# The pool branch's input weights multiplied once with its four 128x128 matrices, in block 1's routing

## The chip, the cores and the metric

The kernel runs on one core of a Trainium2 chip. The metric is the device time of one execution in microseconds. The core's engines run side by side, each with its own queue: TensorE (PE, with its weight loads as PEld), VectorE (DVE), ScalarE (ACT), GpSimd (POOL) and SyncE (SP). They wait for each other through semaphores. A matmul of 32-bit floats shows as two passes in the trace, one through plain transposes as one.

## The reference, cut to what matters

Two transformer blocks work on 1024 tokens of width 1024. Block 1 is a short-convolution mixer and an expert-choice layer: each of 16 experts takes the 128 tokens with the largest affinities. Block 2 is a mixer of two branches and a layer of 32 experts with two choices for each token. Between the blocks the rows are normalized and modulated again. The change concerns the second mixer's pool branch, 512 of its 2056 input columns:

```python
def pool_group(p, w_pool, b_pool, pool_scale):      # p = (h @ w_in)[..., COL_P:IN_COLS]
    ...
    pooled = (cs[:, 1:] - lo) / count[None, :, :, None] - pf
    y = jnp.einsum('bsgc,gcd->bsgd', pooled, w_pool)
    y = (y + b_pool) * pool_scale
```

`cs` is the running sum along the tokens. So each of four groups of 128 columns gets, at every token, the mean over the last 2, 4, 8 or 16 tokens less the token's own value, then a product with that group's 128x128 matrix, a bias and a scale. The pooling works along the tokens and the matrix along the columns, so the two can change places, and the matrix can be multiplied into the input weights.

## The kernel before, in words

The engines' programs are written out by hand, one queue each; every dependency is a counted semaphore. Matrix products are taken as three products of numbers split in two parts (`three`, lines 2513, 2514 and 2516), the parts made by ScalarE (a copy to the high part) and VectorE (the difference). Weights pass through `ring`, 12 slots of 128x1024 floats (512 KB), filled by SP in the order of use.

*Block 1's routing.* The logits of the 16 experts are done at the end of the first output stage. TensorE transposes the affinities (line 2702). VectorE then picks the 128 best tokens of each expert in 16 rounds of three instructions on 32 rows of 512 (lines 1856 to 1859), and signals `top_ready`. Meanwhile SP has loaded six sums over products with the second modulation weights into `xz[:, 2:8]` (line 596), and TensorE adds up their columns, 48 products with one column of ones (line 2526), each group of eight counted on `mod_mm`, up to 12. Then its queue goes on as follows:

```python
pe.wait_ge(S["top_ready"], 1 + past["top_ready"])
pe.transpose(ps[:, 2, 0:2 * E1], top_v[:], ident[0:2 * E1, 0:2 * E1])
pe.transpose(ps[:, 2, 2 * E1:4 * E1], top_f[:], ident[0:2 * E1, 0:2 * E1]).then_inc(S["topT_tr"], 1)
```

VectorE joins the two halves of the tokens (lines 1862 to 1877), GpSimd gathers the rows of the first two experts (line 815), TensorE transposes them (line 2722), and the first expert product starts. ScalarE has copied the first six expert weight chunks (line 1248) before, and does its row copy (line 1177) after the search. SP refills a ring slot when VectorE has split it (line 616).

*The second mixer.* Twelve input projections of 128 columns for all tokens (`n` = 0 to 11, chunks m = 4 to 15) run on TensorE; the work of four heads and the pool branch is put between their pieces by `between(n, k)`. Chunks 8 to 11 are the pool branch's columns of `w_in_2`. ScalarE copies such a projection into `tA` (line 1417), GpSimd makes the window sums and the difference (`pool_sums`, `pool_difference`, counted on `branch`), TensorE multiplies with the group's matrix (`pool_product`, line 2858), and VectorE adds the bias and scales (`pool_back`, line 2160). The four products stand here:

```python
if (n, k) in ((9, 2), (10, 2), (10, 5), (11, 2)):
    pool_product({(9, 2): 0, (10, 2): 1, (10, 5): 2, (11, 2): 3}[n, k])
```

The last projections (n = 8 to 11) are gates: ScalarE takes their sigmoid (lines 1424 and 1426), VectorE multiplies it in (line 2214). The output projection follows when all rows are there (`hy_done`, `pool_out`).

## Time and profile before

| | |
|---|---|
| time, three runs | 2093.75, 2094.17, 2098.7 us (median 2094.17) |
| profiled execution | 2094.59 us, span 2092.9 us |
| mean granted TensorE clock | 0.986 of full |
| busy share of the span | TensorE 96%, its weight loads 80%, VectorE 82%, ScalarE 59%, GpSimd 22% |
| routing of block 1 | from 435 to 484.6 us |
| block 1's experts | from 484.6 to 1036.8 us |
| second mixer's projections | up to 1299.4 us |

Times in the trace are microseconds from the span's start. A row of the timeline gives start, duration, engine, line, operation, output and inputs, and in brackets how long the engine was idle before and what released it. A count (x16) stands for instructions of one kind merged into a row.

### The profile page before, as it was taken

What the parts mean: (1) busy time and instruction counts of PE and PEld (TensorE: products, weight loads), DVE (VectorE), ACT (ScalarE), POOL (GpSimd) and SP (SyncE); (2) the same over time, 40 slices, a digit from 0 to 9 for tenths busy, and PEclk for the clock granted to TensorE, in tenths of its full rate; (3) what the DMA queues carried; (4) which work ended last, traced back from release to release, by engine and by line L of the source; (5) the groups of instructions that cost most, each with busy time, mean ns of one, the idle gap of its engine ahead of it and who ended that gap; (6) DMA issues with size and microseconds to landing.
All of it is one profiled execution on the core that took longest, in us unless ns stands there. A gap on an engine that the chain in (4) does not pass through costs nothing.

```text
span 2092.9 us, 31539 instructions
## 1 busy us (share of the span) xinstructions
PE 2013.9 (96%) x9666; PEld 1664.8 (80%) x9666; DVE 1707.5 (82%) x1929; ACT 1230.5 (59%) x1438; POOL 450.2 (22%) x370
## 2 busy tenths in 40 slices
PE   4999999968999999999999999999999999999997
PEld 4888887867888888888788887888888888887875
DVE  6575756588999999999865555658999999999996
ACT  5311103226888888888654533224888888888874
POOL 2000001101000000000010353111444444443443
PEclk9999999969999999999999999999999999999999
DMA  9476754358999999999821112356999999999997
GB/s 356 133 238 235 242 209 151 119 213 313 387 391 401 391 398 390 399 391 390 310 68 50 51 41 108 114 194 225 385 383 384 375 379 373 370 382 367 375 357 286
DMA packets 201559, 592.66 MB, mean 283 GB/s; under 512 B 24045, under 2 KB 61185, under 8 KB 201484
## 3 DMA queue, kind: packets, MB, share of 16 engines
q1 hardware_dynamic: 177632, 527.50, 66.3%
q0 software_dynamic: 22784, 61.46, 10.1%
q10 hardware_dynamic: 1068, 2.73, 0.3%
q8 instruction: 43, 0.70, 0.1%
q14 instruction: 32, 0.26, 0.0%
HBM read 561.10 MB, written 50.91 MB: 292 GB/s over the span
## 4 chain that ended last, share of the span: by engine, by line
PE 78%; DMA 9%; DVE 8%; ACT 2%; issue 2%; POOL 1%; DVEq 0%; POOLq 0%; ACTq 0%; SPq 0%
PE ps L2513 23%; PE ps L2516 23%; PE ps L2514 23%; DMA ring<-in_w_expert_up 6%; DVE mL L2337 2%; DMA ring<-in_ada_w 1%; PE ps L3038 1%; DMA ring<-in_w_expert_down 1%; PE ps L2634 1%; PE ps L2733 1%; DVE mL L2421 1%; PE ps L2722 1%; PE ps L2682 1%; ACT mH L1466 1%; PE ps L2858 1%
## 5 line engine op out<-in xcount | busy, mean ns | idle before, releaser
L2337 DVE TENSOR_TENSOR mL<-ring,mH 128x1024 fp32r<-128x1024 f32 x384 | 479.2, 1289 | 22.3 <-ACT mH L1466 20.8
L1884 DVE TENSOR_TENSOR mL<-ring,mH 128x1024 fp32r<-128x1024 f32 x384 | 456.5, 1222 | 19.0 <-ACT mH L1248 5.0
L1248 ACT ACTIVATE mH<-ring 128x1024 fp32r<-128x1024 f32 x384 | 401.8, 1060 | 97.3 <-PE ps L2516 86.9
L2513 PE MATMUL ps<-mH,xsH 128*128 128x512 f32 x1072 | 433.6, 404 | 2.8 <-DVE mL L2337 1.4
L1466 ACT ACTIVATE mH<-ring 128x1024 fp32r<-128x1024 f32 x384 | 394.9, 1056 | 65.6 <-PE ps L2516 23.7
L2514 PE MATMUL ps<-mL,xsH 128*128 128x512 f32 x1072 | 417.9, 390 | 0.0
L2516 PE MATMUL ps<-mH,xsL 128*128 128x512 f32 x1072 | 376.8, 391 | 0.0
L2516 PEld LDWEIGHTS ps<-mH,xsL 128*128 128x128 f32 x1072 | 201.2, 188 | 45.0
L2513 PEld LDWEIGHTS ps<-mH,xsH 128*128 128x128 f32 x1072 | 201.7, 188 | 41.5 <-DVE mL L2337 1.6
L2514 PEld LDWEIGHTS ps<-mL,xsH 128*128 128x128 f32 x1072 | 202.0, 188 | 37.3
L951 POOL TENSOR_TENSOR xz<-xz,gate_ffn_row 128x340 f32<-128x340 f32 (+1 forms) x93 | 162.9, 1756 | 239.5 <-DVE mL L2337 220.2
L2513 PE MATMUL ps<-mH,hidH 128*128 128x512 f32 x512 | 200.9, 392 | 1.3 <-issue 1.3
L2514 PE MATMUL ps<-mL,hidH 128*128 128x512 f32 x512 | 200.2, 391 | 0.0
L2516 PE MATMUL ps<-mH,hidL 128*128 128x512 f32 x512 | 158.5, 391 | 0.0
L2513 PE MATMUL ps<-hH,wH 128*128 128x512 f32 x384 | 151.4, 394 | 3.4 <-DVE hL L1636 2.4
L2514 PE MATMUL ps<-hL,wH 128*128 128x512 f32 x384 | 149.5, 389 | 0.0
L2516 PE MATMUL ps<-hH,wL 128*128 128x512 f32 x384 | 122.2, 389 | 0.0
L1582 DVE SCALAR_TENSOR_TENSOR acc<-ring,silu_c,acc 128x1024 f32<-128x1024 f32 x83 | 106.6, 1284 | 16.6 <-DMA ring<-in_ada_w 9.4
L2513 PEld LDWEIGHTS ps<-mH,hidH 128*128 128x128 f32 x512 | 96.8, 189 | 22.5 <-issue 1.9
L2516 PEld LDWEIGHTS ps<-mH,hidL 128*128 128x128 f32 x512 | 96.7, 189 | 20.3
L2514 PEld LDWEIGHTS ps<-mL,hidH 128*128 128x128 f32 x512 | 96.8, 189 | 20.0
L2513 PE MATMUL ps<-woH,zs 128*128 128x512 f32 x256 | 103.0, 402 | 4.1 <-DVE woL L1589 2.6
(507 smaller groups left out, 3139.2 us busy)
## 6 DMA issues: line engine op xcount, KB each, us to landing
ring<-in_w_expert_gate SPq DMA_DIRECT2D x140, 512.0 KB, 11.2
ring<-in_w_expert_up SPq DMA_DIRECT2D x140, 512.0 KB, 11.4
ring<-in_w_expert_down SPq DMA_DIRECT2D x140, 512.0 KB, 12.2
ring<-in_moe_w_gate SPq DMA_DIRECT2D x128, 512.0 KB, 6.4
ring<-in_moe_w_up SPq DMA_DIRECT2D x128, 512.0 KB, 6.3
ring<-in_moe_w_down SPq DMA_DIRECT2D x128, 512.0 KB, 7.6
ring<-in_ada_w SPq DMA_DIRECT2D x96, 512.0 KB, 7.0
ring<-in_sc_w_in SPq DMA_DIRECT2D x24, 512.0 KB, 8.7
```

Source lines behind the costliest of these rows:

```text
L951: pool.tensor_tensor(dst[:, at], src[:, at], gate_ffn_row[:, at], ALU.mult).then_inc(S["m2_row"], 1)
L1248: act.activation(mH[:, wset, :], ring[:, slot, :], ACT.Copy).then_inc(S["m1_hi"], 1)
L1466: act.activation(mH[:, wset, :], ring[:, slot, :], ACT.Copy).then_inc(S["m2_hi"], 1)
L1582: ins = dve.scalar_tensor_tensor(out=acc[:], in0=slot, scalar=silu_c[:, silu_col + k:silu_col + k + 1], in1=acc[:], op0=ALU.mult, op1=ALU.add)
L1884: dve.tensor_tensor(mL[:, wset, :], ring[:, slot, :], mH[:, wset, :].bitcast(F32), ALU.subtract).then_inc(S["m1_lo"], 1)
L2337: dve.tensor_tensor(mL[:, wset, :], ring[:, slot, :], mH[:, wset, :].bitcast(F32), ALU.subtract).then_inc(S["m2_lo"], 1)
L2421: dve.tensor_tensor(mL[:, c % WSETS, :], ring[:, c, :], mH[:, c % WSETS, :].bitcast(F32), ALU.subtract).then_inc(S["m2_lo"], 1)
L2513: pe.matmul(o, high, rh, start=start, stop=False)
L2514: pe.matmul(o, high, rl, start=False, stop=False)
L2516: last = pe.matmul(o, low, rh, start=False, stop=stop)
L2634: last = pe.transpose(ps[:, 4 + c // 4, (c % 4) * P:(c % 4 + 1) * P], xt[:, 1 - r, c * P:(c + 1) * P], ident[:])
L2682: last = pe.matmul(ps[0:2 * width, 7, 0:2 * P], rs[:, k, :], h2P[:, k, :], start=k == 0, stop=k == KD - 1)
```

## The change

The product of the pool branch's input weights (1024x512) with its four matrices is made once, on chip. After the column sums of block 1's routing, ScalarE loads the weights into `xz[:, 2:6]` (four transfers of 512 KB) and the matrices into `acc`. For each of the four groups TensorE transposes the eight 128x128 pieces, ScalarE copies them, TensorE multiplies them with the group's matrix, and ScalarE copies the result back over the weights. At the end ScalarE writes the 2 MB into a new DRAM tensor, `fold_dram`. TensorE waits for the last copy (`fold_ev`) before it goes on to `top_ready`. ScalarE waits for the write (`fold_out`) before the first expert's silu, which overwrites a part of `xz`; SP waits for it before it loads chunk 8.

In the second mixer the chunks 8 to 11 come from `fold_dram`. `pool_product`, its semaphore, its tile `wp` and GpSimd's load of the matrices are gone, and `pool_back` works in place on the window difference, as soon as GpSimd has made it. The rest of the diff shares the new semaphores with old ones.

```diff
--- before.py
+++ after.py
@@ -35,7 +35,7 @@
     silu_ready half_sum sq_done mod_ready tr_ready tr_hi split_hi f_part cv_done c_copied route1 e1_exp m1_used m1_hi
     m1_xT m1_xT_hi slots_ready m1_silu m1_hT m1_hT_hi if_zero gate_in if_hi v_even gate_exp branch d2_out uc_ready 
     q_mm pm_ready pv hn_tr num_out final_in dve_steps cols_tr mod_mm xn_done
-    tr_lo sums_out sums2_out sums_in row_cols row_tr row_copied rows_out rows_here c_here mid_tr tr_mid v_mm pool_steps neg_out mb_in mask_done exp_done small_ready small_exp sq_out intra_out kt_mm kw_out st_mm c_ready hd_out cell_w ov_l close_mm close_act close_dve last_root last_out m2_row m2_dst rows_known aff_ready halves_out affT_tr m1_xT_lo m1_hid m1_hT_lo if_lo v_odd if_mm pool_mm qk_mm qk_out s_mm
+    tr_lo sums_out sums2_out sums_in row_cols row_tr row_copied rows_out rows_here c_here mid_tr tr_mid v_mm pool_steps neg_out mb_in mask_done exp_done small_ready small_exp sq_out intra_out kt_mm kw_out st_mm c_ready hd_out cell_w ov_l close_mm close_act close_dve last_root last_out m2_row m2_dst rows_known aff_ready halves_out affT_tr m1_xT_lo m1_hid m1_hT_lo if_lo v_odd if_mm qk_mm qk_out s_mm
     hn_ready q_out
 """
 
@@ -100,6 +100,7 @@
     neg_dram = dram("neg_dram", [4, T])
     sums_dram = dram("sums_dram", [6, P, D])
     rows_dram = dram("rows_dram", [2, 4, D])
+    fold_dram = dram("fold_dram", [D, 4 * P])
 
 
     ring = sb("ring", [P, RING, D])
@@ -221,7 +222,6 @@
     tB = sb("tB", [P, T], scope=two)
     num = sb("num", [P, NT, P + 1], scope=two)
     cst = sb("cst", [P, NT - 1, P + 1], scope=two)
-    wp = sb("wp", [P, 4, P], scope=two)
     sm = sb("sm", [P, 2, 3, NT], scope=two)
     ms = sb("ms", [P, 8, NT], scope=two)
     gcol = sb("gcol", [P, 3, NT, 4], scope=two)
@@ -266,11 +266,12 @@
 
 
     lines = [
-        [("x1_done", NT), ("x1_done_2", NT)],
+        [("x1_done", NT), ("fold_out", 16), ("x1_done_2", NT)],
         [("sq2", NT), ("sq2_2", NT), ("sq_final", NT + 1)],
         [("var2", NT), ("var2_2", NT), ("var_final", NT + 1)],
         [("rstd2", NT), ("rstd2_2", NT), ("rstd_final", NT + 1)],
         [("h2_out", 16 * NT), ("h2_out_2", 16 * NT)],
+        [("sums_in", 96), ("fold_in", 16 * 5)],
         [("row_cols", 1), ("row_cols_2", 1)],
         [("row_tr", 1), ("row_tr_2", 1)],
         [("row_copied", 1), ("row_copied_2", 1)],
@@ -310,9 +311,10 @@
         [("sq_done", NT), ("sq_done_2", NT)],
         [("xn_done", NT), ("xn_done_2", NT)],
     ]
-    lines += [[(name, NT), (name + "_2", NT)]
-              for name in ("h2_done", "y_ready", "zs_hi", "zs_lo", "rt_done")]
-    lines += [[(name, NT + 1), (name + "_2", NT + 1)] for name in ("tr2", "h2T_ready")]
+    lines += [[(name, NT), (name + "_2", NT)] for name in ("h2_done", "zs_lo", "rt_done")]
+    lines += [[("y_ready", NT), ("fold_mm", 4), ("y_ready_2", NT)], [("zs_hi", NT), ("fold_ev", 4), ("zs_hi_2", NT)]]
+    lines += [[("tr2", NT + 1), ("fold_tr", 4), ("tr2_2", NT + 1)],
+              [("h2T_ready", NT + 1), ("fold_T", 4), ("h2T_ready_2", NT + 1)]]
     lines += [[(name, 2 * KD), (name + "_2", 2 * KD)] for name in ("tr_ready", "tr_hi", "tr_lo")]
     past = {}
     for line in lines:
@@ -442,6 +444,9 @@
     x1_tiles = x1_dram.rearrange("(t p) d -> p t d", p=P)
     h2_tiles = h2_dram.rearrange("(t p) d -> p t d", p=P)
 
+    fold_rows = fold_dram.rearrange("(k p) n -> p k n", p=P)
+    fold_w = xz[:, 2:6, :].rearrange("p u (k n) -> p (u k) n", n=4 * P)
+    fold_T, fold_by = xz[:, 6, :], acc[:, 0:4 * P].rearrange("p (h e) -> p h e", h=4)
     w_in2, w_out2 = (io[n].rearrange("(k p) n -> p k n", p=P) for n in ("w_in_2", "w_out_2"))
     m2_g, m2_u = (io[n].rearrange("e (p k) n -> e p (k n)", p=P) for n in ("w_expert_gate_2", "w_expert_up_2"))
     m2_d = io["w_expert_down_2"].rearrange("e (k p) n -> e p k n", p=P)
@@ -638,8 +643,10 @@
             sp.wait_ge(S["m1_lo"], 24 * E1 - NT + t + 1)
             sp.dma_start(x1_rows[t], x1_tiles[:, t, :]).then_inc(x_in[t], 16)
         for m in range(4, 16):
-            first = (0, FIRST_P, FIRST_O)[(m - 4) // 4] + (m % 4) * P
-            d2_chunk(m, w_in2[:, :, first:first + P], P)
+            first = (0, 0, FIRST_O)[(m - 4) // 4] + (m % 4) * P
+            if m == 8:
+                sp.wait_ge(S["fold_out"], 16 + past["fold_out"])
+            d2_chunk(m, (fold_rows if m // 4 == 2 else w_in2)[:, :, first:first + P], P)
         for k in range(KD):
             d2_chunk(16 + k, w_out2[:, k, :], D)
         sp.wait_ge(S["hy_done"], 4)
@@ -900,7 +907,7 @@
 
         pool.wait_ge(S["m1_lo"], 24 * E1)
         pool.wait_ge(S["tr_ready_2"], 16 + past["tr_ready_2"])
-        for dst, name in ((wq, "w_q_2"), (wk, "w_k_2"), (wp[:], "w_pool_2")):
+        for dst, name in ((wq, "w_q_2"), (wk, "w_k_2")):
             pool.dma_start(dst, io[name].rearrange("h d e -> d h e")).then_inc(S["cell_w"], 16)
         head_mask(0)
         for n in range(3, 9):
@@ -1264,6 +1271,19 @@
 
         for c in range(WSETS):
             m1_hi(0, 0, c)
+        act.wait_ge(S["mod_mm"], 12)
+        for u in range(4):
+            act.dma_start(fold_w[:, 2 * u:2 * u + 2, :], w_in2[:, 2 * u:2 * u + 2, FIRST_P:FIRST_P + 4 * P]
+                          ).then_inc(S["fold_in"], 16)
+        act.dma_start(fold_by, io["w_pool_2"].rearrange("h d e -> d h e")).then_inc(S["fold_in"], 16)
+        for g in range(4):
+            act.wait_ge(S["fold_tr"], g + 1 + past["fold_tr"])
+            act.activation(fold_T.rearrange("p (a b) -> p a b", a=2), ps[:, 4:6, :], ACT.Copy).then_inc(S["fold_T"], 1)
+            act.wait_ge(S["fold_mm"], g + 1 + past["fold_mm"])
+            act.activation(fold_w[:, :, g * P:(g + 1) * P], ps[:, 2:4, :].rearrange("p a (k n) -> p (a k) n", n=P),
+                           ACT.Copy).then_inc(S["fold_ev"], 1)
+        act.wait_ge(S["fold_ev"], 4 + past["fold_ev"])
+        act.dma_start(fold_rows, fold_w).then_inc(S["fold_out"], 16)
         row_copy("_2")
         act.wait_ge(S["slots_ready"], 1)
         for j in range(2):
@@ -1280,6 +1300,7 @@
                 if c in (14, 15) and not (static(q) and s >= E1 - 1):
                     x_hi(s + 1, 1 - r, c - 14)
                 if c == 5 and static(q) and s == 1:
+                    act.wait_ge(S["fold_out"], 16 + past["fold_out"])
                     swiglu_gate(0, 16)
                 if c == 21 and not (static(q) and s == E1):
                     swiglu_gate(s, n - 5)
@@ -2155,9 +2176,8 @@
                                      op0=ALU.mult, op1=ALU.add).then_inc(S["hd_out"], 1)
 
         def pool_back(g):
-            bank = 4 + 2 * (g % 2)
-            dve.wait_ge(S["pool_mm"], g + 1)
-            dve.tensor_scalar(xz[:, 4 + g, :].rearrange("p (a b) -> p a b", a=2), ps[:, bank:bank + 2, :],
+            dve.wait_ge(S["branch"], 5 + g)
+            dve.tensor_scalar(xz[:, 4 + g, :], xz[:, 4 + g, :],
                               col("b_pool_2", g), col("pool_scale_2", g), ALU.add, ALU.mult).then_inc(S["pool_out"], 1)
 
         dve.wait_ge(S["masks"], 7)
@@ -2704,6 +2724,19 @@
         pe.wait_ge(S["sums_in"], 96)
         for part in range(6):
             sum_columns(6 + part, xz[:, 2 + part, :])
+        pe.wait_ge(S["fold_in"], 16 * 5 + past["fold_in"])
+        for g in range(4):
+            if g:
+                pe.wait_ge(S["fold_ev"], g + past["fold_ev"])
+            for k in range(KD):
+                last = pe.transpose(ps[:, 4 + k // 4, (k % 4) * P:(k % 4 + 1) * P], fold_w[:, k, g * P:(g + 1) * P], ident[:])
+            last.then_inc(S["fold_tr"], 1)
+            pe.wait_ge(S["fold_T"], g + 1 + past["fold_T"])
+            for k in range(KD):
+                last = pe.matmul(ps[:, 2 + k // 4, (k % 4) * P:(k % 4 + 1) * P], fold_T[:, k * P:(k + 1) * P],
+                                 fold_by[:, g, :], start=True, stop=True)
+            last.then_inc(S["fold_mm"], 1)
+        pe.wait_ge(S["fold_ev"], 4 + past["fold_ev"])
         pe.wait_ge(S["top_ready"], 1 + past["top_ready"])
         pe.transpose(ps[:, 2, 0:2 * E1], top_v[:], ident[0:2 * E1, 0:2 * E1])
         pe.transpose(ps[:, 2, 2 * E1:4 * E1], top_f[:], ident[0:2 * E1, 0:2 * E1]).then_inc(S["topT_tr"], 1)
@@ -2869,7 +2902,7 @@
             last.then_inc(S["gate_cols"], 1)
 
         def pair_transposes():
-            pe.wait_ge(S["cell_w"], 48)
+            pe.wait_ge(S["cell_w"], 32)
             pe.wait_ge(S["gate_in"], 1 + past["gate_in"])
             pe.wait_ge(S["gate_rows"], 1 + past["gate_rows"])
             for u, w in enumerate((wq, wk)):
@@ -2943,16 +2976,6 @@
             for t in range(NT):
                 last = pe.transpose(ps[:, 6 + t // 4, (t % 4) * P:(t % 4 + 1) * P], num[:, t, 0:P], ident[:])
             last.then_inc(S["hn_tr"], 1)
-
-        def pool_product(g):
-            pe.wait_ge(S["branch"], 5 + g)
-            if g == 0:
-                pe.wait_ge(S["num_out"], 12)
-            elif g == 1:
-                pe.wait_ge(S["hd_out"], 4)
-            else:
-                pe.wait_ge(S["pool_out"], g - 1)
-            pair_matmul(4 + 2 * (g % 2), wp[:, g, :], xz[:, 4 + g, :]).then_inc(S["pool_mm"], 1)
 
         VALUES_AT, BACK_AT = ((1, 2, 3), (1, 4, 5)), {8: 2, 9: 6}
 
@@ -2975,8 +2998,6 @@
                 head_inputs(n - 3)
             if k == 7 and 0 <= n - 3 < 4:
                 head_keys(n - 3)
-            if (n, k) in ((9, 2), (10, 2), (10, 5), (11, 2)):
-                pool_product({(9, 2): 0, (10, 2): 1, (10, 5): 2, (11, 2): 3}[n, k])
 
         pe.wait_ge(S["ones_col"], 1 + past["ones_col"])
         for n in range(12):
```

## Rows read from the trace of the kernel before

**Rows 1.** The page's part 4, the chain that ended last, by engine.

```profile
PE 78%; DMA 9%; DVE 8%; ACT 2%; issue 2%; POOL 1%; DVEq 0%; POOLq 0%; ACTq 0%; SPq 0%
```

**Rows 2.** Timeline of block 1's routing, TensorE's rows.

```profile
442.31 20.64 PE L2526 MATMUL ps<-ones,xz 128*128 128x1 f32 x96 [6.07 <-DMA xz<-sums_dram]
472.93 0.31 PE L2708 MATMUL ps<-ident,top_v 32*128 32x32 f32 x1 [9.98 <-DVE top_f L1860]
473.75 1.01 PE L2713 MATMUL ps<-best,flip 128*128 128x16 f32 x4 [0.41 <-DVE best L1862]
474.77 4.90 PE L2521 MATMUL ps<-ones 128*128 128x128 f32 x28
...
484.62 0.50 PE L2513 MATMUL ps<-mH,xsH 128*128 128x512 f32 x1 [0.59 <-DVE xsL L1890]
```

**Rows 3.** Windows in the routing: length, busy by engine, granted clock, DMA share, GB/s.

```profile
440.00:445.00 5.00, 2.69 (x13) 2.69 (x13) 4.79 (x12) 1.22 (x2) 0.00 (x0) 0.50 1.03 419
...
463.00:472.90 9.90, 0.00 (x0) 0.00 (x0) 9.42 (x22) 0.00 (x0) 0.00 (x0) 0.50 0.00 0
```

**Rows 4.** Chain in order of time, end of the second mixer: start, duration, what.

```profile
1262.88 1.72 PE ps L2858 x4
...
1270.06 0.87 PE ps L2944 x8
...
1299.33 0.28 ACT tB L1426
```

**Rows 5.** Timeline of the second mixer's end on the other engines.

```profile
1267.09 1.23 DVE L2147 TENSOR_TENSOR num<-num,ms 128x1024 f32<-128x1024 f32 x1
...
1273.53 1.20 POOL L895 TENSOR_TENSOR xz<-edge,tA 128x16 f32<-128x16 f32 x1
...
1286.71 1.03 ACT L1424 ACTIVATE tA<-ps 128x1024 f32<-128x1024 f32 x1 [12.39 <-PE ps L2516]
...
1292.52 1.34 DVE L2160 TENSOR_SCALAR xz<-ps,cols 128x1024 f32<-128x1024 f32 x1 [6.06 <-PE ps L2858]
```

**Rows 6.** Instructions of line 904; groups of ScalarE by form, 1160 to 1300.

```profile
L904 POOL DMA_DIRECT2D wp<-in_w_pool x1: 772/772/772, 1078.0 to 1078.0; - x1
...
L1298 ACT ACTIVATE uH<-ring 128x1024 fp32r<-128x1024 f32 x7 | 7.6, 1089 | 6.7 <-PE ps L2516 6.7
```

**Rows 7.** Issues: ScalarE's at the opening, SP's from 1100, gathers of line 815.

```profile
2.35 1.02 ACTq L1083 DMA_DIRECT2D xz<-in_x  x2
...
ring<-in_w_in SPq DMA_DIRECT2D x7, 512.0 KB, 4.0
...
xt<-x_dram SPq DMA_DIRECT2D x1, 512.0 KB, 3.3
...
DMA to landing us min/median/max: 5.7/5.8/9.1
```

**Rows 8.** Timeline in the second mixer; the last row from its groups by form.

```profile
1196.14 1.96 PE L2858 MATMUL ps<-xz,ring 128*128 128x512 f32 x4
...
1198.14 1.03 ACT L1383 ACTIVATE ring<-ps 128x1024 f32<-128x1024 f32 x1 [7.13 <-PE ps L2858]
...
1199.33 1.03 PE L2898 MATMUL ps<-ident,xz 128*128 128x128 f32 x8
...
1213.03 1.95 PE L2906 MATMUL ps<-ring,xz 128*128 128x128 f32 x16
...
L1417 ACT ACTIVATE tA<-ps 128x1024 f32<-128x1024 f32 x5 | 5.3, 1067 | 3.4 <-POOL xz L895 3.4
```

**Rows 9.** Timeline of TensorE at the kernel's opening.

```profile
27.72 3.54 PE L2540 MATMUL ps<-ident,xz 128*128 128x128 f32 x16 [2.37 <-ACT xz L1111]
...
31.32 1.73 PE L2521 MATMUL ps<-ones 128*128 128x128 f32 x14
```

**Rows 10.** Window of block 1's experts (columns as above); waits in it: us, times, longest.

```profile
484.60:1036.80 552.20, 552.18 (x2552) 456.69 (x2552) 525.02 (x505) 441.67 (x457) 44.11 (x29) 1.00 1.01 384
...
ACT mH L1248 <- PE ps L2516: 86.9, 293, 2.0
```

## The prediction

> **What bounds the kernel now.** I read the page first, for its chain of work that ended last: TensorE is 78% of it, GpSimd 1% [rows 1]. So time is won or lost where TensorE's work changes while it is on that chain, or where the chain leaves TensorE and something new is put into it. The change does one of each, so I followed the chain in order of time through both places and then read the timelines there.
>
> The first place is block 1's routing, a serial stretch. VectorE searches for the largest affinities, round after round. TensorE does its 48 column sums beside the search, from 442.31 to 462.95, then idles 9.98 us, until VectorE's last result lets it transpose the winners at 472.93 [rows 2]. From there each step up to the first expert product at 484.62 waits for the one before. In the idle stretch the transfers stand still too [rows 3]: the ring of expert weights is full.
>
> The second place is the end of the second mixer. From 1262 to 1299 the chain is TensorE without a break, and the four pool products are four pieces of it, 1.72 us each, the first at 1262.88 [rows 4]. VectorE and ScalarE wait for TensorE there, not the other way round [rows 5].
>
> **The change, part by part.**
>
> *Removed: the four products.* Four pieces of 1.72 us on the chain are 6.9 us [rows 4]. What is late next? Transposing the last head's rows needs VectorE's result of 1268.32 (1267.09 + 1.23); TensorE would come to it at 1270.06 - 1.72 = 1268.34, just in time [rows 4, 5]. GpSimd's last window difference ends at 1274.7. ScalarE's third gate copy follows TensorE: three products earlier it starts at 1281.5 in place of 1286.71, and what VectorE and ScalarE do behind it (some 5 us) is done near 1286.5, while TensorE would end at 1299.33 - 6.9 = 1292.4 [rows 5]. So nothing takes the products' place. As a lower bound I let one of them (1.72) turn into a wait at the marginal transposes: 5.2 to 6.9 us, and I take 6.9. VectorE's four pool steps no longer wait for a product; that is worth nothing, since TensorE's projections cover it: VectorE idled 6.06 us before the last of them [rows 5].
>
> *Moved at no cost.* GpSimd's load of the pool matrices goes, 0.77 us of its issue [rows 6]; GpSimd is hardly on the chain, and were it, these 0.8 us would be the gain. The input chunks 8 to 11 come from the folded copy, in the same runs of 512 bytes; ScalarE's splits of such chunks waited for TensorE alone, never for a transfer [rows 6]. If that cover failed, one late chunk would cost up to the 4.0 us of its landing [rows 7]. SP's new wait there is for a write that will have ended hundreds of microseconds before.
>
> *Added: the loads.* ScalarE waits for all column sums, so nothing is issued before 463.0, with only the 9.9 us of the idle stretch left [rows 2]. Behind this wait on its queue stands its row copy, which follows the search anyhow. Five transfers go out; two issues of ScalarE's take 1.02 us [rows 7], so the last one leaves near 465.6. A lone 512 KB load lands in 3.3 us; at the 419 GB/s that the engines reach, its bytes are 1.25 of these, so some 2.0 us are fixed [rows 3, 7]. The four big loads (2.10 MB) take 5.1 us at 410 GB/s; the pool matrices (0.26 MB in runs of 512 bytes) take 1.0, since a chunk of twice that size in such runs lands in 4.0 us [rows 7]. That makes 463.1 + 2.0 + 5.1 + 1.0 = 471.2; I take 471.3. Bounds: everything at 419 GB/s gives 470.7; the slowest landing of the gathers, 9.1 us [rows 7], counted from the last issue, gives 474.7.
>
> *Added: the fold.* Its four groups run strictly one after another, because every hand-over is a wait: eight transposes, a copy of 128x1024, eight products of 128x128, another copy. The second mixer has each of them at full clock: transposes 1.03, copies 1.03 and 1.07, the sixteen passes of eight such products 1.95, hand-over to ScalarE 0.04 (1198.10 to 1198.14), back to TensorE 0.16 (1199.17 to 1199.33) [rows 8]. A group is 1.03 + 0.04 + 1.03 + 0.16 + 1.95 + 0.04 + 1.07 + 0.16 = 5.48 us. At half clock eight transposes cost 3.54 / 2 = 1.77 [rows 9] and a pass 20.64 / 96 = 0.215 [rows 2], sixteen of them 3.44; the group is then 7.71 us.
>
> Which clock? The granted clock is 0.50 in the idle stretch [rows 3], which is 1.2 GHz. After the search, the 28 passes from 474.77 took 4.90 us, 0.175 each: they began at half clock and ended at full [rows 2]. At the kernel's opening 16 transposes ran at half rate (0.22 each), and the 14 passes behind them at full (0.12) [rows 9]. So I take the first group at half clock and three at full: 7.71 + 16.44 = 24.2 us. Bounds: 21.9 (all full) and 30.8 (all half). The Trainium skill ("TensorE: Matmul & The Clock Gate", Part 4: PE-mode transpose) says that transposes do not bring the clock to its full level. By that only the products would help here, and the sum would lean to the slow rival below; the opening's rows speak against it.
>
> *The wait that this puts into the chain.* The fold ends at 471.3 + 24.2 = 495.5. On TensorE's queue the winners' transposes stand behind it, so they go from 472.9 to 495.5, 22.6 us later. For them wait VectorE's choice of tokens, ScalarE's row copy, GpSimd's gather and SP's refill of the ring, so all shift alike. Of the 9.9 us that the search still covers, the loads use 8.3.
>
> *After it.* The small products from 472.93 to 474.76 run at full clock: half of 1.01, and 0.1 on the two before, are 0.6 us gained [rows 2]. The folded matrix is written out (2.10 MB, some 5 us) just as the gather starts. Gathers in this stretch landed in 5.7, 5.8 and 9.1 us [rows 7], so 0 to 3.3 us more; I take 1.0, as most of the write is done before the gather's data moves. ScalarE's wait for that write, ahead of the first silu, is hidden behind 16 weight chunks of 552.2 / 384 = 1.44 us, 23 us of TensorE work [rows 10]; if it were not, the rest of the 5 us would show.
>
> *Sum*, against the profiled execution's own 2094.6: 22.6 - 0.6 + 1.0 - 6.9 = +16.1, 2110.7. The median shown, 2094.2, is 0.4 us lower; I say 2110.
>
> **The rivals.**
> - *The clock stays at half through the fold.* The copies leave TensorE idle 2.5 of a group's 7.7 us, and 20 us of column sums did not lift the clock [rows 2, 3]; the opening speaks against it. The fold is 30.8 us and the 0.6 is lost: 471.3 + 30.8 - 472.9 = 29.2, and 2094.6 + 29.2 + 1.0 - 6.9 = 2117.9. The skill's rule on transposes leads here.
> - *The clock is up from the first group*: 2.2 us less, 2108.5.
> - *The gather pays the whole 3.3* beside the write: 2113.0.
> - *The mixer's end does not move*, because another engine was as late as TensorE: 2110.7 + 6.9 = 2117.6. The waits of VectorE and ScalarE [rows 5] say no.
> - *Not slower: block 1's experts give the delay back.* If that stage waited for weights, a later start would find more of them ready, and only the mixer's gain would be left: 2087.7. It decides once the stage holds 16.1 us of TensorE idle time that weights cause. The trace has 0.02 us of idle time in 552.2, and ScalarE's weight copies wait for TensorE, 86.9 us in all [rows 10]; and with the ring full nothing can be fetched ahead.
>
> **How the numbers follow.** My forecast has 0.55, half clock 0.16, full clock from the start 0.11, the gather 0.09, the unmoved end 0.04, the delay given back 0.03, and 0.02 is for something unseen near no change. The unknowns at their ends together give 2094.6 + (470.7 + 21.9 - 472.9) - 0.6 - 6.9 = 2106.8 and 2094.6 + (474.7 + 30.8 - 472.9) + 3.3 - 5.2 = 2125.3. The far upper end needs every term at its worst, so I cut it, and give 2105 to 2119. A measurement of this kernel tells some 0.3%, 6 us, from no change. All the slow cases lie beyond that: slower 0.95, same 0.02, faster 0.03.
>
> **What would show it.** In the profile after: the last of the five loads landing near 471; transposes, copy, products, copy, four times between 471 and 495, the first round longer; the winners' transposes near 495 and the first expert product near 507; an experts' stage as long as before; no products between the pieces of the last projections, and a mixer some 6.9 us shorter. I am wrong if the fold ends before 480, if the experts' stage is shorter than its 552 us, or if the last projections wait for VectorE or GpSimd.

## The result, and the profile after

The changed kernel takes 2119.05 us (median of four runs, 2115.82 to 2121.23), 1.0111 times the kernel before (95% interval 1.0099 to 1.0124): some 23 us slower, where I forecast 16 and a range that ended at 2119. A fourth run of the kernel before, at 2279.01 us, is left out of the comparison as slow. The profiled execution was its fastest, 2115.82 us with a span of 2114.2, so 21.2 us over that of before.

The page's chain by engine, in answer to [rows 1]:

```profile
PE 77%; DMA 11%; DVE 7%; ACT 3%; issue 2%; POOL 0%; SPq 0%; ACTq 0%; DVEq 0%; POOLq 0%
```

The share of transfers has grown from 9% to 11%: in order of time the chain now passes through the fold's loads (the last one, of the matrices, for 6.9 us) and through a longer gather (9.2 us). The timeline of TensorE in the routing, in answer to [rows 2] (lines 2732 and 2736 are the fold's transposes and products, 2741 the winners' transposes, 2755 those of the gathered rows, 2533 the first expert product):

```profile
470.39 1.97 PE L2732 MATMUL ps<-ident,xz 128*128 128x128 f32 x8 [9.14 <-DMA acc<-in_w_pool]
473.47 3.78 PE L2736 MATMUL ps<-acc,xz 128*128 128x128 f32 x16 [1.11 <-ACT xz L1281]
478.37 1.10 PE L2732 MATMUL ps<-ident,xz 128*128 128x128 f32 x8 [1.11 <-ACT xz L1283]
480.57 3.31 PE L2736 MATMUL ps<-acc,xz 128*128 128x128 f32 x16 [1.11 <-ACT xz L1281]
485.00 1.09 PE L2732 MATMUL ps<-ident,xz 128*128 128x128 f32 x8 [1.11 <-ACT xz L1283]
487.20 2.05 PE L2736 MATMUL ps<-acc,xz 128*128 128x128 f32 x16 [1.11 <-ACT xz L1281]
...
495.74 0.24 PE L2741 MATMUL ps<-ident,top_v 32*128 32x32 f32 x1 [1.11 <-ACT xz L1283]
...
508.14 1.94 PE L2755 MATMUL ps<-ident,xz 128*128 128x128 f32 x8 [6.22 <-DMA xz<-h_dram,tok_in]
...
510.70 0.79 PE L2533 MATMUL ps<-mH,xsH 128*128 128x512 f32 x1
```

The four rounds are there: transposes, copy, products, copy, with 1.11 us of idle TensorE at every hand-over. They last from 470.39 to the winners' transposes at 495.74, 25.35 us. A round at half clock is 1.97 + 3.78 us of TensorE work, one at full clock 1.09 + 2.05. In this execution the second round is mixed: its transposes ran at full clock and most of its products at half. The winners' transposes come at 495.74, 22.8 us later than before. From them to the first expert product it is 14.96 us, where it was 11.69 [rows 2]. The windows show the granted clock (last but two of the columns) in the idle stretch, in the fold and in the gather's wait, then over the experts:

```profile
465.00:470.00 5.00, 0.00 (x0) 0.00 (x0) 4.76 (x12) 0.00 (x0) 0.00 (x0) 0.50 0.96 350
475.00:480.00 5.00, 3.35 (x19) 2.81 (x18) 0.00 (x0) 1.52 (x2) 0.00 (x0) 0.73 0.00 0
480.00:485.00 5.00, 3.31 (x17) 3.02 (x17) 0.00 (x0) 1.54 (x2) 0.00 (x0) 0.66 0.00 0
485.00:490.00 5.00, 3.14 (x24) 2.71 (x24) 0.00 (x0) 1.73 (x2) 0.00 (x0) 1.00 0.00 0
...
505.00:510.00 5.00, 1.86 (x9) 1.89 (x10) 0.04 (x1) 0.60 (x1) 0.00 (x0) 0.50 0.99 401
...
510.70:1063.30 552.60, 552.60 (x2554) 457.11 (x2552) 524.89 (x505) 441.58 (x458) 44.12 (x29) 1.00 1.00 382
```

The transfers that stood still between 463 and 472.9 [rows 3] now carry the loads. TensorE is busy in every microsecond of the experts' stage, as in [rows 10]: nothing is given back there. The clock is at half again when the gathered rows arrive (505 to 510): their eight transposes take 1.94 us and the first expert product 0.79, where it took 0.50 [rows 2]. The timelines of ScalarE and GpSimd, and the transfers issued from 495 to 511 (median us from issue to landing at the end):

```profile
461.29 2.17 ACTq L1276 DMA_DIRECT2D xz<-in_w_in  x4
...
495.72 0.38 ACTq L1286 DMA_DIRECT2D fold_dram<-xz  x1
...
498.83 1.84 POOL L822 DMA_INDIRECT xz<-h_dram,tok_in  x1 [0.54 <-DVE tok_in L1921]
...
1319.21 0.28 ACT L1447 ACTIVATE tB<-ps 128x128 f32<-128x128 f32 x1 [7.51 <-PE ps L2536]
```

```profile
fold_dram<-xz ACTq DMA_DIRECT2D x1, 2048.0 KB, 7.7
...
xz<-h_dram,tok_in POOLq DMA_INDIRECT x2, 9.4
```

The write is issued at 495.72 and lands 7.7 us later, at 503.4. The gather issued at 498.83 runs beside it, and TensorE can use its rows only 9.3 us after the issue. In the kernel before it was 6.0 us:

```profile
476.55 1.84 POOL L815 DMA_INDIRECT xz<-h_dram,tok_in  x1 [0.45 <-DVE tok_in L1900]
...
482.52 1.07 PE L2722 MATMUL ps<-ident,xz 128*128 128x128 f32 x8 [2.85 <-DMA xz<-h_dram,tok_in]
```

So the 3.3 us from the winners to the first expert product are 3.3 for the gather and 0.5 for what follows its rows at half clock, less 0.5 for the small products ahead of it. The mixer's end is the last copy of a gate, 1319.21. From the first expert product to it are 808.5 us, against 814.7 before [rows 2, 4]: 6.2 us gained.

### The profile page after: what moved, and what is told of

Same layout as the page of the kernel before. It is cut to its first block, busy times and chain, and to the rows that moved or that the text cites. A ratio compares the mean times of both kernels' runs of the same rounds, so it can differ in the third digit from the quotient of the medians.

```text
span 2114.2 us, 31729 instructions
## 1 busy us (share of the span) xinstructions
PE 2023.1 (96%) x9746; PEld 1676.5 (79%) x9746; DVE 1707.6 (81%) x1929; ACT 1238.3 (59%) x1446; POOL 451.5 (21%) x369
## 4 chain that ended last, share of the span: by engine, by line
PE 77%; DMA 11%; DVE 7%; ACT 3%; issue 2%; POOL 0%; SPq 0%; ACTq 0%; DVEq 0%; POOLq 0%
PE ps L2533 23%; PE ps L2536 22%; PE ps L2534 22%; DMA ring<-in_w_expert_up 6%; DVE mL L2357 2%; PE ps L2546 1%; DVE mL L2441 1%; DMA ring<-in_ada_w 1%; PE ps L3059 1%; DMA x_dram<-xz,tok_out 1%; DMA ring<-in_w_expert_down 1%; PE ps L2755 1%; PE ps L2766 1%; PE ps L2702 1%; PE ps L2654 1%
## 5 line engine op out<-in xcount | busy, mean ns | idle before, releaser
L2357 DVE TENSOR_TENSOR mL<-ring,mH 128x1024 fp32r<-128x1024 f32 x384 | 480.3, 1292 | 21.7 <-ACT mH L1487 20.3
```

The lines of the kernel that those rows point to most:

```text
L2357: dve.tensor_tensor(mL[:, wset, :], ring[:, slot, :], mH[:, wset, :].bitcast(F32), ALU.subtract).then_inc(S["m2_lo"], 1)
```

## The experiments

Theory A: the change loses some 26 us in the routing (the fold on the chain, partly at half clock, and a gather slowed by the write) and gains some 6.5 at the mixer's end, independently of each other; my forecast missed by the clock and the gather alone. Its rivals stand in the expectations, as theory B.

### The changed kernel twice more

No edit.

> The changed kernel, unaltered. Theory A: how much of the fold runs at half clock differs from execution to execution (25.3 us in the profile that I have, with half of it at full clock; 29.6 and 30.9 in the profiles of two kernels with the same fold), and this is what spreads the changed kernel's times over 5.4 us: the fold of this profiled execution is 25 to 31 us long, its time is higher where the fold is longer, by about as much, and the median is 2117 to 2120. Theory B: the fold is always near 25.3 us in this kernel and the spread has another source: its length is 25.0 to 25.7 again.

Measured: 2120.12 us (2116.98 to 2122.48), ratio 1.0122 [1.0106, 1.0137]. The median is just over theory A's 2120. The profile again fell on the fastest execution, 2116.98, with a fold of 25.3 us (472.06 to 497.38), which both theories allow. So it decides nothing, and I took one more.

> The changed kernel once more, unaltered, since the second profile of it fell on its fastest execution of four, as the first did (2115.82 and 2116.98, both with a fold of 25.3 us). Theory A: the length of the fold goes with the time of the execution: if this one takes 2119 us or more, its fold is 28 to 31 us long, and if it takes under 2118, 25 to 26. Theory B: the fold is 25 to 26 us even in an execution of 2119 us or more.

Measured: 2120.78 us (2117.11 to 2123.78), ratio 1.0120 [1.0103, 1.0137]. This profile is that of the slowest execution, 2123.78. TensorE's timeline and two windows of it:

```profile
473.15 1.97 PE L2732 MATMUL ps<-ident,xz 128*128 128x128 f32 x8 [9.45 <-DMA acc<-in_w_pool]
476.23 3.78 PE L2736 MATMUL ps<-acc,xz 128*128 128x128 f32 x16 [1.11 <-ACT xz L1281]
481.12 1.97 PE L2732 MATMUL ps<-ident,xz 128*128 128x128 f32 x8 [1.11 <-ACT xz L1283]
484.20 3.78 PE L2736 MATMUL ps<-acc,xz 128*128 128x128 f32 x16 [1.11 <-ACT xz L1281]
...
497.07 1.10 PE L2732 MATMUL ps<-ident,xz 128*128 128x128 f32 x8 [1.11 <-ACT xz L1283]
499.28 3.67 PE L2736 MATMUL ps<-acc,xz 128*128 128x128 f32 x16 [1.11 <-ACT xz L1281]
504.06 0.24 PE L2741 MATMUL ps<-ident,top_v 32*128 32x32 f32 x1 [1.11 <-ACT xz L1283]
```

```profile
490.00:495.00 5.00, 3.89 (x18) 3.48 (x18) 0.00 (x0) 1.02 (x1) 0.00 (x0) 0.50 0.00 0
495.00:500.00 5.00, 2.77 (x16) 2.24 (x16) 0.00 (x0) 2.05 (x2) 0.00 (x0) 0.84 0.00 0
```

The same instructions took 30.9 us (473.15 to 504.06), nearly all at half clock. The fold is 5.6 us longer than in the first profile, and it starts 2.8 later; the two executions' times differ by 8.0. The work is the same: TensorE's eight pieces add up to 16.4 us in the first profile and to 22.0 here, and the eight waits are 1.11 us in both. Theory A holds for these three profiles. The mean granted clock of the twelve executions of the three sets fits it: 0.983 or 0.984 in the three under 2118 us, 0.979 to 0.982 in the nine others.

### The two terms put right, one by one and together

```diff
+        busy(1, 28)
         pe.wait_ge(S["fold_in"], 16 * 5 + past["fold_in"])
...
             last.then_inc(S["fold_tr"], 1)
+            busy(1, 3)
...
             last.then_inc(S["fold_mm"], 1)
+            busy(1, 3)
...
-        busy(1, 14)
+        busy(1, 36)
```

> The changed kernel with idle TensorE time filled by products of ones that nobody reads: 28 before the fold's first transposes, 3 behind each eight transposes and each eight products, 36 in place of 14 in the gather's wait. Theory A: the first group and most of the second ran at half clock; with the clock up the four groups take 5.4 us each, 21.9 in place of 25.3, the gathered rows' transposes 1.07 in place of 1.94, and the first expert products start at full clock: 4 to 5 us less than the changed kernel. Theory B: hand-overs and copies set the fold's pace, or fillers do not raise the clock: no gain, or up to 2 us of loss where a filler is still running when the next piece could start.

Measured: 2113.48 us (2113.16 to 2117.81), ratio 1.0092 [1.0079, 1.0105]. The fold is 22.5 us (473.20 to 495.71), the gathered rows' transposes 1.35. Four of the five times lie within 0.7 us, the fifth 4 us above. Filling idle time with work that nobody needs makes the kernel faster, by 4 to 6 us going by the ratios and 6 to 7 going by the medians. One part of theory A failed: the first expert product still began at half clock.

```profile
509.54 0.79 PE L2533 MATMUL ps<-mH,xsH 128*128 128x512 f32 x1
```

```diff
-        act.dma_start(fold_rows, fold_w).then_inc(S["fold_out"], 16)
         row_copy("_2")
         act.wait_ge(S["slots_ready"], 1)
         for j in range(2):
             x_hi(0, 0, j)
+        act.dma_start(fold_rows, fold_w).then_inc(S["fold_out"], 16)
```

> The changed kernel with the 2 MB write of the folded matrix issued behind ScalarE's copies of the first gathered rows, so that no write runs beside the first gather. Theory A: the write made the gather land 9.2 us after its issue in place of 5.8; here it lands in 5.8 again, the first expert product comes 3.4 us earlier, and the kernel takes 3.4 us less than the changed one (ratio to the kernel before 1.0095 in place of 1.011). Theory B: the gather is slow for another cause (for instance that the queues had stood still): it lands in 9 us still, no change.

Measured: 2115.29 us (2111.72 to 2121.93), ratio 1.0095 [1.0082, 1.0108]. The times spread over 10.2 us. The fold is as it was, and 30.9 us long in the profiled execution, the slowest (2121.93). Rows of TensorE's and GpSimd's timelines there:

```profile
501.96 0.24 PE L2741 MATMUL ps<-ident,top_v 32*128 32x32 f32 x1 [1.11 <-ACT xz L1283]
...
505.04 1.84 POOL L822 DMA_INDIRECT xz<-h_dram,tok_in  x1 [0.48 <-DVE tok_in L1921]
...
512.15 1.94 PE L2755 MATMUL ps<-ident,xz 128*128 128x128 f32 x8 [4.02 <-DMA xz<-h_dram,tok_in]
...
514.71 0.79 PE L2533 MATMUL ps<-mH,xsH 128*128 128x512 f32 x1
```

The gather's rows were there after 7.1 us in place of 9.3, and winners to first product take 12.75 us in place of 14.96. In this trace the late write was worth 2.2 us, not 3.4. One trace is not enough for its price, since the first gather varies without any write: 6.0 us in the kernel before, 7.7 in the kernel without products below. Over all profiles it took 8.6 to 9.8 us with the write beside it (seven profiles, 9.4 on average) and 5.8 to 7.7 without (seven, 6.4). So the write costs it some 3.0 us.

Both edits in one kernel:

> The changed kernel with both: filling products that keep the clock up through the fold and the gather's wait, and the 2 MB write behind ScalarE's copies of the gathered rows. Theory A: the forecast of 2110 missed by two terms alone, the clock in the fold and the gather beside the write; with both put right the time is 2109 to 2111.5 (2113.5 with the fillers alone, less 2.2 to 3.4). Theory B: something else is still in the difference, or the two are the same microseconds: 2113 or more.

Measured: 2111.18 us (2109.11 to 2112.43), ratio 1.0071 [1.0057, 1.0085]. TensorE's timeline:

```profile
472.71 1.09 PE L2733 MATMUL ps<-ident,xz 128*128 128x128 f32 x8 [1.85 <-DMA acc<-in_w_pool]
...
474.91 2.05 PE L2738 MATMUL ps<-acc,xz 128*128 128x128 f32 x16 [0.44 <-ACT xz L1281]
...
494.20 0.24 PE L2744 MATMUL ps<-ident,top_v 32*128 32x32 f32 x1 [0.44 <-ACT xz L1283]
...
505.57 0.50 PE L2533 MATMUL ps<-mH,xsH 128*128 128x512 f32 x1 [0.59 <-DVE xsL L1911]
```

All four rounds run at full clock: 21.5 us, by my lower bound 21.9. Winners to first product are 11.37 us, where they were 11.69 before the change. The time is in theory A's range and within 1.2 us of the forecast, but that does not show that the two terms missed alone. This fold is 2.7 us shorter than the 24.2 of my sum and the gather pays nothing of its 1.0, so the sum would be 2110.7 - 2.7 - 1.0 = 2107.0. The other 4.2 us lie in the start of the fold (472.71 for 471.3: 1.4), the small products (0.3), the mixer (809.15 us from the first expert product to the last gate copy: 1.3) and what stands behind it (1.2).

### Loss and gain apart

The fold with the second mixer of before (the old chunks, tile, load, `pool_product` and `pool_back`):

> The fold is made and written out in the routing as in the changed kernel, but the second mixer is that of the kernel before: it loads the plain input columns and makes its four pool products. Theory A: the changed kernel's time is the sum of a loss of 26 to 27 us in the routing and a gain of 6.7 us at the mixer's end, which do not touch each other. Then this kernel is about 27 us over the kernel before (some 2121 us), 6 to 7 us slower than the changed kernel, and its mixer is as long as before. Theory B: part of the loss sits in the second mixer (the folded weights' loads, or waits that took the products' place). Then this kernel is no slower than the changed one, within 2 us.

Measured: 2125.49 us (2120.34 to 2128.43), ratio 1.0136 [1.0121, 1.0151], 4.7 to 6.4 us over the changed kernel's three medians. That is 4 us over the expected 2121; the profiled execution, the slowest, has a fold of 29.6 us. Its last gate copy:

```profile
1332.33 0.28 ACT L1446 ACTIVATE tB<-ps 128x128 f32<-128x128 f32 x1 [3.26 <-PE ps L2536]
```

From the first expert product at 516.91 to it are 815.4 us, as long as before. Theory A, with a gain a little under the expected.

The kernel before without `pool_product`, with `pool_back` in place, and no fold:

> The kernel before without the four pool products and their matrices (the pool branch goes unmultiplied, with bias and scale alone), and without any fold. Theory A: 6.7 us (four pieces of 1.72 less a wait of 0.2 at the last head's transposes) come off the chain, none of it taken back: 2087.5 us, ratio 0.997. Theory B: another engine is nearly as late as TensorE at the mixer's end, so that the time stays within 2 us of the kernel before.

Measured: 2109.52 us (2105.1 to 2111.99), ratio 1.0063 [1.0051, 1.0075], slower than before. Neither theory said that. From the first expert product (485.49) to the last gate copy (1294.57) it took 809.1 us, 5.6 less than before, so the mixer did gain. But the pool branch's output had other values, and with them block 2's choice of experts. The page's transfer issues of this kernel:

```profile
ring<-in_w_expert_gate SPq DMA_DIRECT2D x144, 512.0 KB, 11.0
```

The kernel before and the changed one load 140 such chunks, and as many of the two other kinds. One more block of 12 chunks went through, by my estimate some 17 us at the 1.44 us that a chunk takes in block 1. In the trace the stretch behind the last gate copy is 20.3 us longer than before (813.8 against 793.6). The first gather was slow here too, 7.7 us with no fold and no write:

```profile
475.67 1.84 POOL L814 DMA_INDIRECT xz<-h_dram,tok_in  x1 [0.45 <-DVE tok_in L1899]
...
483.39 1.24 PE L2720 MATMUL ps<-ident,xz 128*128 128x128 f32 x8 [4.57 <-DMA xz<-h_dram,tok_in]
```

A part left out ahead of a router changes the work behind it; the total can't be compared, only the stretch up to there.

### Where the fold can stand

Eight half groups in place of four groups, with the next transposes issued ahead of the products:

```diff
+            fold_turn(first)
+            for h in range(first, end):
+                if h + 1 < end:
+                    fold_turn(h + 1)
+                fold_times(h)
```

> The changed kernel with the fold in eight half groups: the next four transposes are issued ahead of four products, with two buffers of half the size, so that TensorE works while ScalarE copies. The same products and loads. Theory A: hand-overs and copies leave TensorE idle for 2.5 us or more of each group, and this idleness also keeps the clock down. Without them the fold takes 13 to 17 us (eight steps of 1.5 us at full clock, the first two at half, and a tail of 1.5), so the kernel takes 9 to 14 us less than the changed one: 2105 to 2110. Theory B: the clock stays at half whatever the density: eight steps of 2.9 us and the tail, 24.5 us, the kernel takes 1 to 6 us less than the changed one.

Measured: 2106.74 us (2103.26 to 2108.19), ratio 1.0052 [1.0039, 1.0066]. The fold took 13.5 us (471.00 to 484.53). Its windows:

```profile
470.00:475.00 5.00, 4.00 (x19) 3.77 (x20) 1.15 (x4) 1.30 (x3) 0.00 (x0) 0.53 0.02 5
475.00:480.00 5.00, 5.00 (x47) 5.00 (x46) 0.00 (x0) 4.24 (x8) 0.00 (x0) 1.00 0.00 0
```

Without the gaps the same products were at full clock from 475 on, to the end of the fold. Theory A.

Loads into other memory, issued once the sums have landed, the fold group by group as in the changed kernel:

```diff
+    fold_x = sb("fold_x", [P, 6, D], scope=early_in)
...
+        act.wait_ge(S["sums_in"], 96)
+        act.wait_ge(S["stored"], 1)
+        for u in range(4):
...
         for c in range(WSETS):
             m1_hi(0, 0, c)
-        act.wait_ge(S["mod_mm"], 12)
```

> The changed kernel with the weights and matrices loaded into other memory (that of the first expert's rows), right behind the sums' loads near 443, and the fold as before, group after group. Theory A: the loads set the fold's start, 9.1 us behind the column sums; now it starts with the end of the sums near 461.5 and ends near 487 to 492, and the kernel takes 8 to 9 us less than the changed one (2110), still 15 over the kernel before. Theory B: the earlier loads push back the sums' loads or the expert weights, or the fold lasts longer without the pause: less than 5 us gained.

Measured: 2111.72 us (2110.99 to 2114.99), ratio 1.0077 [1.0064, 1.0091]. The fold started 0.8 us after the column sums; in the profiled execution, the slowest, it took 28.2 us:

```profile
464.19 1.97 PE L2737 MATMUL ps<-ident,fold_x 128*128 128x128 f32 x8 [0.82 <-DMA fold_x<-in_w_pool]
```

The gain of 7 to 9 us is theory A's, though the fold began 2.7 us later than it said.

Both together, all eight half groups ahead of the winners' transposes, and the late write:

> The split kernel with all eight half groups ahead of the winners' transposes, and the 28 filling passes back behind them. Theory A: only idle time that is really there hides the fold: its start near 463.5 and eight steps, the first three at half clock (some 9 us) and five at 1.35, with a tail of 1.3, set its end near 480, so the winners' transposes come 7 to 8 us later than in the kernel before: 2094 to 2097. Theory B: where the fold stands matters little once its loads are early and it is dense: 2088 to 2090.

Measured: 2093.62 us (2090.78 to 2098.31), ratio 0.9989 [0.9980, 0.9998]. The time lies just under theory A's range, well over theory B's.

```profile
475.99 0.24 PE L2771 MATMUL ps<-ident,top_v 32*128 32x32 f32 x1 [0.69 <-ACT xz L1291]
...
479.07 1.84 POOL L826 DMA_INDIRECT xz<-h_dram,tok_in  x1 [0.54 <-DVE tok_in L1938]
...
484.87 1.94 PE L2785 MATMUL ps<-ident,xz 128*128 128x128 f32 x8 [4.34 <-DMA xz<-h_dram,tok_in]
```

The fold ran from 462.21 to 475.99, so the winners' transposes came 3.1 us later than before, not 7 to 8: only the transposes of the first two half groups and the products of the first ran at half clock throughout. The gather, with no write beside it, took 5.8 us. Some 2 us are left of the mixer's gain, less than the 6 us that I had said a measurement tells from no change.

The same with four half groups ahead, and four in place of the 28 passes that fill the gather's wait:

```diff
         row_transpose(1)
-        busy(1, 14)
+        fold_products(4, 8)
```

> Early loads, half groups, four of the eight ahead of the winners' transposes and four in place of the 28 passes that fill the gather's wait; the 2 MB write goes behind ScalarE's copies of the gathered rows. All results as before. Theory A: the change lost only because its fold stood on the chain; here nearly all of it lies in idle time, the first expert product starts within 3 us of the kernel before, and the mixer's 6.7 us remain: 2087 to 2091. Theory B: the routing has no room for 13 to 25 us of TensorE work, or ScalarE's copies delay its row copy and the gathered rows: 2094 or more.

Measured: 2087.83 us (2085.84 to 2088.84), ratio 0.9962 [0.9948, 0.9976]: faster than the kernel before by 7 us, and than the changed one by over 31. TensorE's timeline:

```profile
463.34 1.97 PE L2749 MATMUL ps<-ident,fold_x 128*128 128x128 f32 x8 [0.82 <-DMA fold_x<-in_w_pool]
...
472.80 0.25 PE L2772 MATMUL ps<-ident,top_v 32*128 32x32 f32 x1 [0.69 <-ACT xz L1291]
...
478.11 2.06 PE L2758 MATMUL ps<-fold_x 128*128 128x128 f32 x16
481.71 1.06 PE L2786 MATMUL ps<-ident,xz 128*128 128x128 f32 x8 [1.53 <-DMA xz<-h_dram,tok_in]
...
483.81 0.50 PE L2551 MATMUL ps<-mH,xsH 128*128 128x512 f32 x1 [0.59 <-DVE xsL L1929]
```

The winners' transposes stand where they stood before (472.93), the second half is done 1.5 us before the gathered rows arrive, and the first expert product is 0.8 us earlier than before (0.7 of it between the winners' transposes and it).

The same fold, unread, with the second mixer of before:

> The kernel with early loads, half groups, the fold split about the search's end and the late write, but with the second mixer of the kernel before: plain input columns and the four pool products; the folded copy is made and not read. Theory A: that fold is free (the first expert product came 0.8 us earlier than in the kernel before), and the whole gain of 7 us over the kernel before was the mixer's: here 2093 to 2096, within 1.5 us of the kernel before, 6 to 7 us over the split kernel. Theory B: part of the gain came from the routing, where TensorE's clock was already up at the first expert product: 2090 to 2092.

Measured: 2095.38 us (2093.2 to 2099.0), ratio 0.9999 [0.9990, 1.0008]. The fold so placed is free within the interval, and the mixer's end is worth the 7.5 us between the medians of these two kernels. Their profiles have 6.5 us of it between the first expert product and the last gate copy, 815.8 us here (482.49 to 1298.26) and 809.3 in the split kernel (483.81 to 1293.09):

```profile
1298.26 0.28 ACT L1464 ACTIVATE tB<-ps 128x128 f32<-128x128 f32 x1 [3.26 <-PE ps L2554]
...
1293.09 0.28 ACT L1465 ACTIVATE tB<-ps 128x128 f32<-128x128 f32 x1 [7.51 <-PE ps L2554]
```

## Why the prediction missed

The direction stood, and so did the path: the fold ahead of the winners' transposes, everything behind it shifted, the experts' stage as long as before, the products gone from the mixer's end. Two terms of the sum were too small, and one of them rested on a clock that I took as the same in every execution. Against the first profile:

| term | forecast | measured |
|---|---|---|
| winners' transposes | +22.6 | +22.8 |
| from there to the first expert product | +0.4 (gather 1.0, small products -0.6) | +3.3 (gather 3.3, small products -0.5, half clock behind it 0.5) |
| experts and second mixer | -6.9 | -6.2 |
| behind it | 0 | +1.3 |
| sum | +16.1 | +21.2 |

That profile is of the fastest execution. The three profiles of the changed kernel are on average 8.2 us over the forecast of 2110.7: 3.0 by the fold (27.2 us for 24.2), 3.0 between the winners and the first expert product, 1.0 by the loads, 0.8 by a mixer that gained 6.1, 0.8 behind it, less 0.4 because the column sums ended earlier.

**The gather.** The step that failed: "I take 1.0, as most of the write is done before the gather's data moves". I priced the write at some 5 us; it took 7.7 and covered 4.6 us of the gather, which took 3.3 us more than before. The rival with the whole 3.3 was right on this term, at a chance of 0.09; its total, 2113.0, lacked the others. The profiles with and without the write put its price at some 3.0 us. Behind it stands what I had not counted: in the gather's wait TensorE idled 6.2 us, where it was 2.85 before, and the clock was at half when the rows came, so that the gathered rows' transposes took 1.94 us, and the first expert products began at half clock. With fillers in that wait and the late write, the first product took 0.50 us again.

**The fold's clock.** The step that failed: "So I take the first group at half clock and three at full". I read one clock for the kernel. The granted clock differs from one execution to the next: 25.3, 25.3 and 30.9 us in three profiles of the changed kernel, 29.6 and 30.9 in two others with the same fold. My forecast and my "half clock" rival were two ends of what one kernel does. The medians lie 3 to 5 us above the first profile, and a longer fold accounts for most of that in the third profile (5.6 of 8.0 us). Had the range taken the half-clock fold together with the whole gather, it would have reached 2120.2 and held the medians of the first two sets.

The rule of the Trainium skill ("TensorE: Matmul & The Clock Gate", Part 4: PE-mode transpose), that transposes do not bring the clock up, comes off better here than the opening's rows [rows 9] had made me think: in the third profile the transposes at 497.07 ran at full clock and the products behind them at half again. Half-us windows show the same order throughout the six profiles whose fold has these gaps: all fifteen rises of the clock come in a round's products or within a us behind them, and all nine falls between the end of a round's transposes and 0.7 us into its products. But no run of mine has transposes alone, and the opening's rise came behind transposes, so the rule is not shown. The same page (Part 1, A second HAM failure mode: psum-queue depth-cycling) tells of a kernel whose clock swings because TensorE idles briefly between groups of products; the windows 0.73, 0.66, 1.00 here, and 1.00 from 475 on in the fold of half groups, whose gaps are gone, agree.

**The rest.** The loads landed 9.1 to 9.5 us after the column sums in place of 8.3, for a reason that no run takes apart; in the first profile the sums ended 1.7 us earlier and hid it. The fold end of 495.5 was so right by two errors against each other: 0.8 us of loads and 1.1 of fold against those 1.7. The experts gave nothing back. From the first expert product to the last gate copy, three profiles with the old mixer took 814.7 to 815.8 us and eleven with the new one 808.5 to 810.9, on average 5.9 less; so the 6.9 of the sum was somewhat too much, and its bounds of 5.2 to 6.9 held. What stands behind that copy took 793.1 to 795.4 us in the thirteen profiles with the same block 2, so the 1.3 us there are no more than its spread from one execution to the next.

## What to carry to other kernels

Work put into a waiting stretch is free only up to the wait's length, hand-overs included: of the fold's 25 to 31 us, 9 were eight waits of 1.11. Ask first whether its inputs can be there at the start of the stretch, whether its steps can overlap, and whether a second wait takes the rest; this turned +23 us into -7. Where a stretch has gaps, price TensorE at both clocks, let the range reach from one to the other, and look at what a large write will run beside before issuing it at the first possible moment.

## What the runs showed that I had not expected

- The same instructions ran 25.3 us in one execution and 30.9 in another, by TensorE's clock alone. The changed kernel's three sets of times spread over 5.4 to 6.7 us, and filling the gaps brought four of five times within 0.7; but the sets of the kernel before, which has no fold, spread over 3.8 to 8.7, so the fold's clock is not the only source. What decides the clock in an execution no run shows. The Trainium skill ("TensorE: Matmul & The Clock Gate", Part 1, What's actually happening) says that the monitor runs freely, not in step with the kernel; no run here shows it.
- Products that nobody reads make a kernel faster by some 4 to 7 us.
- The first gather's rows were there 8.6 to 9.8 us after its issue beside a 2 MB write, and after 5.8 to 7.7 without it.
